# A hybrid decoder step on one core: x tiles loaded at once, norm1 as a row, and a new order around the last token tile

## The reference, cut to what matters

```
xn  = rms_norm(x, norm1)                     # x * rsqrt(mean(x*x) + 1e-5) * norm1
z   = xn @ w_in                              # 1024 x 2312: q,k,v,o and gates of 4 mLSTM heads; q,k,v of 8 attention heads
h   = mlstm_chunked(...)                     # matrix memory with exp input gate, sigmoid forget gate
o   = window attention: softmax(q k^T/8 + rel_bias[t5_bucket(dist)], learned sink) v      # window 128
x   = x + concat(h * m_gain * sigmoid(mo), o) @ w_out
x2  = rms_norm(x, norm2)
top-4 of 32 experts by softmax over x2 @ w_router + b_router
y   = x + sum over chosen experts of gate * (swiglu(x2 @ w_gate[e], x2 @ w_up[e]) @ w_down[e])
out = rms_norm(y, final_norm)
```

## Time and profile before

| | before |
|---|---|
| median of 3 runs (lowest, highest) | 1576.64 us (1576.19, 1577.05) |
| the profiled execution, its own time | 1576.4 us |
| its span in the trace | 1574.6 us |
| TensorE busy | 1473.7 us, 94% |
| VectorE busy | 1284.3 us, 82% |
| ScalarE busy | 1048.9 us, 67% |
| GpSimd busy | 209.0 us, 13% |
| read from and written to HBM | 445.24 MB and 23.39 MB, 298 GB/s over the span |

### The profile page before, as it was taken

The page is one execution under the profiler, slowest core; times in us unless marked ns, Lnnn a source line. Parts: engine busy times, 40 slices in busy tenths (PEclk is TensorE's granted clock), DMA queues, the critical chain, the costliest instruction groups (busy, mean ns, idle before and its releaser), DMA issues.

```text
span 1574.6 us, 22062 instructions
## 1 busy us (share of the span) xinstructions
PE 1473.7 (94%) x7211; PEld 1054.1 (67%) x7211; DVE 1284.3 (82%) x1376; ACT 1048.9 (67%) x991; POOL 209.0 (13%) x190
## 2 busy tenths in 40 slices
PE   2899999893999999999999999999999999999993
PEld 1798864552677777777777777777777777777772
DVE  5234426646899999999999999999999999999996
ACT  3234421341777778777777878787778788777875
POOL 1000001100011211111111122111111111211110
PEclk9999999795999999999999999999999999999997
DMA  7521030334899999999999999999999999999994
GB/s 245 118 88 54 3 126 1 86 122 162 313 367 364 367 365 361 366 377 375 370 366 366 372 363 366 368 364 374 371 371 369 367 369 368 365 366 359 371 363 173
DMA packets 169527, 463.83 MB, mean 295 GB/s; under 512 B 13396, under 2 KB 27352, under 8 KB 169224
## 3 DMA queue, kind: packets, MB, share of 16 engines
q1 hardware_dynamic: 155336, 430.24, 73.3%
q0 software_dynamic: 7392, 21.50, 6.1%
q10 hardware_dynamic: 6768, 11.70, 2.6%
HBM read 445.24 MB, written 23.39 MB: 298 GB/s over the span
## 4 chain that ended last, share of the span: by engine, by line
PE 89%; DMA 4%; DVE 3%; ACT 2%; issue 1%; ACTq 1%; DVEq 0%; POOLq 0%; SPq 0%
PE ps L1567 84%; PE ps L1570 5%; DMA sc_bias<-reg_p 3%; DMA reg_p<-in_w_in 1%; DVE ring_r L432 0%; DMA reg_a<-xhat_rows,slot_tok 0%; DMA y_rows<-reg_a,slot_dst 0%; ACT reg_z L986 0%; ACT ring_r L737 0%; DVE ring L1171 0%; DMA ring<-y_rows 0%; DMA reg_x<-in_x_prompt 0%; DVE reg_z L1506 0%; DVE ring_r L1036 0%; ACT ring L708 0%
## 5 line engine op out<-in xcount | busy, mean ns | idle before, releaser
L1567 PE MATMUL ps<-ring_r,reg_z_r 128*96 128x512 f32 x4608 | 1098.7, 395 | 0.0
L1567 PEld LDWEIGHTS ps<-ring_r,reg_z_r 128*96 128x96 f32 x4608 | 737.8, 162 | 309.4
L432 DVE TENSOR_TENSOR ring_r<-ring,ring_r 128x2048 fp32r<-128x2048 f32 x387 | 875.1, 2287 | 43.2 <-ACT ring_r L906 42.2
L906 ACT ACTIVATE ring_r<-ring 128x2048 fp32r<-128x2048 f32 x387 | 738.8, 1915 | 152.2 <-PE ps L1567 149.1
L648 POOL DMA_INDIRECT reg_a<-xhat_rows,slot_tok x33 | 66.0, 2000 | 1033.5 <-DVE slot_tok L1450 1033.5
L1567 PE MATMUL ps<-reg_a_r,ring_r 128*128 128x260 f32 x576 | 113.3, 292 | 7.1 <-ACT reg_z L747 7.1
L917 ACT ACTIVATE reg_z_r<-ps 128x384 fp32r<-128x384 f32 x130 | 59.5, 484 | 88.5 <-PE ps L1570 88.5
L1567 PEld LDWEIGHTS ps<-reg_a_r,ring_r 128*128 128x128 f32 x576 | 93.8, 195 | 8.2 <-issue 8.2
L656 POOL DMA_INDIRECT y_rows<-reg_a,slot_dst x33 | 75.7, 2294 | 37.6 <-ACT reg_a L939 32.5
L747 ACT ACTIVATE reg_z<-ps 128x260 f32<-128x260 f32 x36 | 13.8, 387 | 89.5 <-PE ps L1567 78.2
L1462 DVE TENSOR_TENSOR reg_z_r<-ps,reg_z_r 128x384 fp32r<-128x384 f32 x130 | 68.6, 548 | 0.0
(11 more groups left out here) (307 smaller groups left out, 999.5 us busy)
## 6 DMA issues: line engine op xcount, KB each, us to landing
ring<-in_w_gate SPq DMA_DIRECT2D x131, 1024.0 KB, 6.7
ring<-in_w_up SPq DMA_DIRECT2D x128, 1024.0 KB, 5.8
ring<-in_w_down SPq DMA_DIRECT2D x128, 1024.0 KB, 7.8
ring<-in_w_in SPq DMA_DIRECT2D x9, 1024.0 KB, 5.2
ring<-in_w_out SPq DMA_DIRECT2D x4, 1024.0 KB, 9.3
reg_x<-in_x_prompt SPq DMA_DIRECT2D x4, 512.0 KB, 4.8
ring<-in_x_prompt SPq DMA_DIRECT2D x4, 512.0 KB, 5.4
xhat_rows<-reg_b ACTq DMA_DIRECT2D x4, 512.0 KB, 3.3
```

What stands on the lines that cost most here:

```text
L432: return eng.tensor_tensor(rest_r(k), w, rounded_r(k).bitcast(F32), ALU.subtract)
L906: act.activation(rounded_r(k), ring[:, slot_of(k), :], ACT.Copy).then_inc(hi_ready, 1)
L1567: return pe.matmul(out, lhsT, rhs, start=start, stop=stop, skip_group_check=True)
```

## The change

Five things change.

1. x goes into five buffers of its own (in reg_z), all loads issued at once. The gate columns, b_if and sinks are loaded on SP's queue instead of ScalarE's; norm2 isn't loaded here any more. `consts_in` now counts three loads: b_if, sinks and m_gain.
2. norm1 is loaded as a row on all partitions (`n1_bc`), and VectorE multiplies by it while it scales the rows. `cols` keeps the four columns of m_gain; their transposition stands before tile 4's.
3. ScalarE rounds the transposed x from PSUM, a half tile in one instruction; VectorE only subtracts. Four PSUM banks take turns instead of two. ScalarE loads its table for the root before x is there.
4. SP waits for the bias write and issues the table's load, behind w_in pieces 3 and 4 and ahead of pieces 5 to 8.
5. At tile 4, VectorE forms the bias remainders and the first weight remainder ahead of `choose(3)`, and the third weight remainder (`split` 2) only after the gate table. TensorE releases pieces 3 to 7 after it has transposed the gathered rows of expert 0.

```diff
-        xbuf = reg_x[:, :].rearrange("p (b n) -> p b n", b=2)
+        xbuf = reg_z[:, 0:NTILE * D].rearrange("p (i n) -> p i n", i=NTILE)
+        n1_bc = reg_x[:, 0:D]
...
             for i in range(NTILE):
-                if i >= 2:
-                    sp.wait_ge(xT_psum, 2 * (i - 1))
-                    sp.wait_ge(rms_ready, i - 1)
-                sp.dma_start(xbuf[0:rows(i), i % 2, :], x_rows(i)).then_inc(x_in[i % 2], 16)
-                if i == 1:
-                    for m in range(3):
-                        load_w_in(m)
+                sp.dma_start(xbuf[0:rows(i), i, :], x_rows(i)).then_inc(x_in[i], 16)
+            sp.dma_start(wif_v, w_in[:, :, GATE_COL:GATE_COL + 8]).then_inc(wif_in, 16)
+            for m in range(3):
+                load_w_in(m)
+            sp.dma_start(b_if, ...).then_inc(consts_in, 16)
+            sp.dma_start(sink_bc, a["sinks"].to_broadcast([P, AH])).then_inc(consts_in, 16)
...
-            for m in range(3, N_IN):
+            load_w_in(3)
+            load_w_in(4)
+            sp.wait_ge(bias_out, 16)
+            skew = bass.AP(sc_bias.tensor, P - 1, [[RLEN - 1, P], [P * RLEN, AH], [1, 2 * P]])
+            sp.dma_start(bias, skew).then_inc(bias_in, 16)
+            for m in range(5, N_IN):
                 load_w_in(m)
...
+            def round_xT(i):
+                r = rows(i)
+                for q in range(2):
+                    n = 2 * i + q
+                    act.wait_ge(xT_psum, n + 1)
+                    act.activation(xnT_hi[:, 4 * q:4 * q + 4, i * P:i * P + r],
+                                   ps[2 + n % 4][:, 0:4 * P]..., ACT.Copy).then_inc(xnhi_ready, 1)
...
-                if j == 2:
-
-                    act.wait_ge(bias_out, 16)
-                    act.dma_start(bias, skew).then_inc(bias_in, 16)
...
-                dve.tensor_scalar(xbuf[0:r, i % 2, :], xbuf[0:r, i % 2, :], ssq[0:r, i:i + 1], None,
-                                  ALU.mult).then_inc(xn_ready, 1)
+                dve.scalar_tensor_tensor(xbuf[0:r, i, :], xbuf[0:r, i, :], ssq[0:r, i:i + 1], n1_bc[0:r, :], ALU.mult,
+                                         ALU.mult).then_inc(xn_ready, 1)
...
+                    if q == 0:
+                        dve.tensor_tensor(xnT_lo_a[:, :, ts], x_ps, hi, ALU.subtract).then_inc(xT_ready, 1)
+                    else:
+                        dve.tensor_tensor(xnT_lo_b[:, :, ts], x_ps[:, 0:3, :], hi[:, 0:3, :], ALU.subtract)
+                        dve.tensor_tensor(xnT_lo_c[:, ts], x_ps[:, 3, :], hi[:, 3, :], ALU.subtract).then_inc(xT_ready, 1)
...
             turn(4)
-            pe.wait_ge(y_ready, 2 * NTILE)
-            tr(ps[1][0:1, 0:1], ident[0:1, 0:1], 1).then_inc(pieces_used, N_FIRST - 8)
             logits_of(4)
...
             transpose_rows(0, 16)
+            pe.wait_ge(y_ready, 2 * NTILE)
+            tr(ps[1][0:1, 0:1], ident[0:1, 0:1], 1).then_inc(pieces_used, N_FIRST - 8)
             pe.wait_ge(gate_list, 1)
```

More of the change, by code:

```diff
@@ L233, in hybrid_step @@
         y_all = ring[:, 0:5, 0:D]
-        xnT_lo = [split_view(region, words, first, [P, TT]) for region, words, first in
-                  [("reg_c", 2304, TT * c) for c in range(4)] + [("reg_b", 2048, TT * c) for c in range(3)]
-                  + [("reg_t", 4120, 3600)]]
+        xnT_lo_a = split_view("reg_c", 2304, 0, [P, 4 * TT])[:, :].rearrange("p (c t) -> p c t", c=4)
+        xnT_lo_b = split_view("reg_b", 2048, 0, [P, 3 * TT])[:, :].rearrange("p (c t) -> p c t", c=3)
+        xnT_lo_c = split_view("reg_t", 4120, 3600, [P, TT])
+        xnT_lo = [xnT_lo_a[:, c, :] for c in range(4)] + [xnT_lo_b[:, c, :] for c in range(3)] + [xnT_lo_c[:, :]]
         gates = sb("gates", [8, TT])
@@ L324, in hybrid_step @@
         pieces_used = sem("pieces_used")
-        x_in = [sem("x_in_0"), sem("x_in_1")]
+        x_in = [sem(f"x_in_{i}") for i in range(NTILE)]
+        n1_in, wif_in, xnhi_ready = sem("n1_in"), sem("wif_in"), sem("xnhi_ready")
         consts_in, relT_in, cache_in = sem("consts_in"), sem("relT_in"), sem("cache_in")
@@ L701, in _ @@
-            act.dma_start(sink_bc, a["sinks"].to_broadcast([P, AH])).then_inc(consts_in, 16)
-            act.dma_start(wif_v, w_in[:, :, GATE_COL:GATE_COL + 8]).then_inc(consts_in, 16)
-            act.wait_ge(eps_made, 1)
-            for i in range(NTILE):
-                act.wait_ge(x_in[i % 2], 16 * (i // 2 + 1))
-                act.activation(ring[0:rows(i), RING + HIS - 1, (i % 2) * D:(i % 2 + 1) * D], xbuf[0:rows(i), i % 2, :], ACT.Square,
+            act.dma_start(n1_bc, a["norm1"].to_broadcast([P, D])).then_inc(n1_in, 16)
@@ L709, in _, with square @@
+            act.dma_start(reg_w[0:4, 0:P], a["m_gain"][0].rearrange("(c p) -> c p", p=P)).then_inc(consts_in, 16)
+            def square(i):
+                act.wait_ge(x_in[i], 16)
+                act.activation(ring[0:rows(i), RING + HIS - 1, (i % 2) * D:(i % 2 + 1) * D], xbuf[0:rows(i), i, :], ACT.Square,
                                accum_out=ssq[0:rows(i), i:i + 1])
                 rms(ssq[0:rows(i), i:i + 1], D).then_inc(rms_ready, 1)
+            def round_xT(i):
[4 more added lines that the diff above has]
+                    act.activation(xnT_hi[:, 4 * q:4 * q + 4, i * P:i * P + r],
+                                   ps[2 + n % 4][:, 0:4 * P].rearrange("p (c t) -> p c t", c=4)[:, :, 0:r],
+                                   ACT.Copy).then_inc(xnhi_ready, 1)
@@ L712, in _ @@
+            act.wait_ge(eps_made, 1)
+            act.activation(small[:, 92:93], lim_col, ACT.Sqrt)
+            square(0)
+            square(1)
+            square(2)
+            round_xT(0)
+            square(3)
+            round_xT(1)
+            square(4)
+            round_xT(2)
+            act.wait_ge(wif_in, 16)
+            act.activation(wif_r[:, 0], wif_v, ACT.Copy).then_inc(w_hi, 1)
+            round_xT(3)
+            round_xT(4)
             act.dma_start(o["s_k"][0, :, 0:WIN - 1], a["cache_k"][0, :, 1:WIN]).then_inc(out_done, 16)
```

78 lines of the change are left out of this document (33 added, 45 removed).

## The result

The median went from 1576.85 us (1576.19 to 1577.23) to 1558.12 us (1555.35 to 1558.43, 4 runs), a ratio of 0.9873 with a 95% interval of 0.9861 to 0.9885. The forecast was 1545.5 with a range of 1538 to 1554. The profiled execution took 1558.03 us, its span 1555.8.

What follows compares the result with a forecast made beforehand. TensorE fills the untouched expert loop, so time can only come from before it: opening 15.0, bias wait 9.4 and last tile 6.7 make 31.1 off 1576.4, 1545.3; the median, 0.24 above, is 1545.5, range 1538 to 1554.

Steps and rivals of the forecast that it cites:

- the bias wait: Projection: ScalarE's wait for the sc_bias write moves to SP, so evacuations continue and first logits come at 72.1; gain 9.4 us.
- A: Rival, projection: the bias table is the new wait, landing at 78 if the write takes 48 us; 1552 us, chance 0.12.
- E: Rival, projection: the wait only changes engine, SP's held blocks 5 to 8 stop TensorE; 1555 us, chance 0.03.
- The opening: Start to first product with a w_in block: all x loads issued at once, 46.3 to 31.3; gain 15.0 us (11 to 17.2).
- The landing, taken at 21: Opening: b_if and sinks land at 21 us behind 5.7 MB on SP's queue, giving a first product at 24.0.
- The last tile: Tile 4, before the expert loop: VectorE's reordering and the later release of weight pieces; gain 6.7 us (4.5 to 7.5).
- the order: Tile 4: with VectorE reordered, the second add waits for TensorE and the copy follows the transposition at once; gain 5.1 us.
- The gather: Tile 4: without the weight pieces beside it, 5.83 becomes 4.2 us, between bounds 5.8 and 3.3; gain 1.6 us.
- C: Rival, expert loop: late pieces and y_rows share DMA engines, the loop pays once, 4 to 8 us; 1551 us, chance 0.07.
- D: Rival, expert loop: it settles in a later phase, each of 32 experts growing by 1.2 us; 1583 us, chance 0.04.
- the cost of 0: Expert loop: pieces 3 to 7, released at 378.7 instead of 366.9, still land before ScalarE wants them; cost 0.

Runs made afterwards that it cites:

- e1: Changed kernel, but the bias rows are written once and SP copies them 128 times DRAM to DRAM ahead of w_in piece 3; 1548.09 us.
- e3: Changed kernel with part 4 undone: the wait for the bias write and the table's load back in ScalarE's queue after block 2; 1564.14 us.
- e5: Changed kernel with all of part 5 undone (VectorE's order at tile 4 and the late release of pieces 3 to 7); 1563.31 us.
- e6: Changed kernel with only the late release of pieces 3 to 7 undone, VectorE's new order kept; 1560.37 us.
- e4: Changed kernel with only b_if and sinks moved back to ScalarE's queue; 1556.75 us in one run.
- e9: Changed kernel with bias rows written once and copied 128 times DRAM to DRAM, and b_if and sinks on ScalarE's queue; 1546.51 us.
- e10: Changed kernel with the old-form bias write issued at about 15 us, and b_if and sinks ahead of it on ScalarE's queue; 1557.20 us.

## Why the prediction was wrong, point by point

**The step that failed is the bias wait: "Gain 9.4, if what is late next isn't later."** It gave 1.0 in the trace. The prediction looked for what is late next among the things that wait for the write by name (the table, SP's held pieces 5 to 8) and gave each a margin. The right candidate doesn't name the write at all; it only shares engines with it. The row was to be had: the issues of the stretch showed a w_in piece at 15.7 us to landing, three times what it takes without that write (5.2 in e1), and the listing of 66 to 70 us a queue with an unfinished load and no packets. The prediction used the 49 GB/s of the write for the write's own length and did not ask what a DMA share of 0.44 at 49 GB/s does to the loads beside it. With piece 3 landing 2 us after the write's end the sum would have been: write issued at 24.0, ended at 63.4, piece 3 at 65.4, and the first logits 15.8 us behind it, as in the kernel after (67.14 to 82.90): 81.2 instead of 72.1. That takes 9.1 of the 9.4 back, and the whole would have been 1554.6. With part 4 undone in the changed kernel (e3) this piece takes 57.38, 7.1 more than before, since TensorE came 12.7 us earlier and the write only 5.7. So part 4 did work; what it won back was what the opening would have lost again.

**Rivals A and E.** The write took 39.15 us (26.03 to 65.18), so its length was as costed. The table landed at about 73.9, and the first logits at 82.90 came right behind the remainder of w_in piece 4 (the prediction's block 4), as it wanted; A is refuted. E put its wait in the right kind of place, a w_in piece, and nearly its price, but for pieces 5 to 8 held on SP; those were never due while SP waited (65.18 against 78.12).

**The opening: 12.7 for 15.0, of which chance is a part.** Four kernels have this opening unchanged beside the kernel after: e1, e3, e5 and e6. The sinks landed between 21.9 and 23.5 in them, and the first w_in block at 34.01, 31.67, 31.65 and 31.84: forecast 31.3. So the term was right to 0.6 us in three of five executions and 2.4 to 2.7 off in two. The landing, taken at 21, was 0.9 to 2.5 low in all; the prediction had no term for the issues, and the sinks were issued only at 15.8 to 16.1. From landing to first product it took 2.3 instead of 3.0, which hid a part. The prediction worked out from the Trainium skill, "DMA: Bandwidth & Descriptors", section "Queues, rings and completion order", that on ScalarE's queue the constants would land near 12 and the sum be 21.8. No row has that landing; in e4, e9 and e10 nothing waits for them when TensorE wants them, at 21.1 to 21.3, which agrees. The first product comes at 23.7 to 23.9, not 21.8, because the norm1 row landed at 10.0 and not by 6.5; VectorE's work behind it took 13.6 instead of 14.8 (10.01 to 23.57 in e4).

**The last tile: 6.7 for 6.7**, and by its terms too: 5.2 for the order up to the gather's issue (5.1) and 1.5 for the gather, 5.83 to 4.33 (1.6). The gather was taken at 4.2; that was a choice between two bounds, and luck has a part in it. The fit of the Trainium skill, same page, section "Anatomy of one DMA", would have had 2.9, and none of the eight late-releasing kernels came near it (4.20 to 4.42).

**The loop (C, D).** From the gather's landing to the end 1190.2 to 1191.2 us in all twelve traces, late release or not. Both refuted; the cost of 0 was right.

**The sum.** 12.7 + 1.0 - 1.2 + 6.7 - 0.4 = 18.8, the difference of the spans. The middle stretch, which no part touches, took 1.2 more, and this is no effect of the change (below).

## What to carry to other kernels

When a wait is to be taken away, list the transfers in flight beside it, not only those that its waiter needs: each with its issue, its landing and the moment at which it is first wanted, shifted by the gain. What lands slowly beside a long small-rowed write is late next, however little it has to do with it. And if moving such a write only changes the victim, make it short: 39 us became 10 when it was rewritten as a copy with 128 outermost.
